# Moving the side work of a hybrid attention block: conditioning items, attention links, row sums and the last tiles of a projection

## The chip, the cores and the metric

The kernel runs on one core of a Trainium2 chip. The metric is the device time of one execution in microseconds (us), smaller is better; the time of a kernel is the median of its runs. A change of 0.3% (6.9 us here) is about what a measurement of this kernel can tell from no change.

## The reference

One layer of a streaming encoder on 512 tokens of width 2048, all in float32:

```python
c_act = silu(c)
shift_m, scale_m, gate_m, shift_f, scale_f, gate_f = split(c_act @ w_ada + b_ada, 6)
h = rmsnorm(x, g_pre_mix) * (1.0 + scale_m) + shift_m
proj = h @ w_in                 # columns: 8 attention heads, 4 gated linear heads, small ones
fox = forgetting attention of 8 heads x 128: causal softmax(q k / sqrt(128) + cum[q] - cum[k]) v
gla = gated linear attention of 4 heads (keys 128, values 256), state read at chunk ends of 64
y = concat(head_rmsnorm(fox), head_rmsnorm(gla) * silu(r)) @ w_out
x = x + gate_m * rmsnorm(y, g_post_mix)
h = rmsnorm(x, g_pre_mlp) * (1.0 + scale_f) + shift_f
x = x + gate_f * rmsnorm(square(relu(h @ w_mlp_in)) @ w_mlp_out, g_post_mlp)
```

`w_ada` is 2048 x 12288, so the conditioning vectors alone read 100 MB.

## The kernel before

It is written engine by engine in program order: every engine (SP issues the DMAs, PE multiplies, ACT is the scalar engine, DVE the vector engine, POOL the GpSimd engine) has its own list of instructions and waits on counting semaphores (`wait_ge(name, value)`). Nothing is scheduled by a planner. The order in each list is fixed by hand through tables of slots.

**Products.** Each float32 operand is split into a high part (ACT copies it to a rounded format, `split_hi`, L1101) and a low part (DVE subtracts, `split_lo`, L1485). A product is three matmuls (L737 to L739): high by high, high by low, low by high. Weights come in tiles `w_raw`, two buffers, so SP may issue tile m only once tile m-2 is split (`slot_free`).

**Groups.** The input projection is eight groups. A group has 16 steps k (eight weight tiles of two k), and a step has six column tiles b, so 288 matmuls. Groups 0 to 3 project two attention heads each, groups 4 to 7 one gated linear head each. While PE works at group r it also does the mixer of group r-1 (so attention runs in groups 1 to 4), in 32 half steps called slots: slot 2k after b=2 and slot 2k+1 after b=5 of step k (`group_steps`). ACT and DVE run the same 32 slots in `group(r, work)`; after every fourth slot they split one weight tile. The mixer of the last gated linear head has no group left: it runs in the first quarter of the output projection (`out_steps(0)`), 32 slots of two (k, t) pairs each.

**Attention (`fox_slot`).** For block j of 8 (two heads, four query blocks): PE makes logits in slot 3j (L811), DVE adds the bias and takes the row maximum (L1590 to L1595), ACT takes the exponential in slot 3j+1 (L1153), PE transposes it in 3j+2 (L821), ACT copies it in 3j+3 (L1163), PE multiplies by the values in 3j+4 (L832), DVE divides and sums squares (`f_o`, L1606, L1608), POOL takes the root (L2116), DVE normalises in 3j+6 (L1613) behind the row maximum of the next block but one, and PE transposes the result in 3j+7 (L841), ahead of the product of the next block. DVE stores it to `cat` (L1625).

**Conditioning items.** The vectors of `w_ada` that the later parts need are summed on DVE from items of 1 MB (two DMAs of 512 KB each, two buffers): eight items in each of groups 1 to 4 (`load_f` L538, `f_item` L1535), four per gated linear head (`load_g` L545, `g_item` L1552). SP's table `F_AT` says after which weight tile of a group an item is issued; DVE's table of the same name says in which slots it is added, two halves per item. SP waits for the addition of item i-2 (`am_used`) before it issues item i. At the end the partial sums are added over partitions by PE: `f_columns` (L774, 16 narrow matmuls) or `g_rows` (L780), and DVE makes the vectors of them (L1523, L1562).

**Seams.** After slot 31 DVE and ACT copy the six finished banks out (`evict_group`, L1496, L1499, L1112). PE's next group needs these copies, bank by bank. In the output projection `out_steps(cg)` takes 16 k by four token tiles t, into banks 0 to 3 and 4 to 7 in turn; in the last quarter (cg = 3) its second half goes tile by tile, so that the normalisation of tile 0 can begin early. It ends in a chain over four token tiles (L1313, L1858, L2078, L1884, L1324, L1342, L1862), before which the MLP cannot start (L1008).

## Time and profile before

| | |
|---|---|
| median of 3 runs | 2312.89 us (2312.43 to 2318.76) |
| the profiled execution: its own time | 2309.94 us |
| the profiled execution: span from first to last instruction | 2307.9 us |
| PE busy | 2173.3 us, 94% of the span |
| DVE busy | 1520.3 us, 66% |
| ACT busy | 850.8 us, 37% |
| start and group 0 | 0 to 177.8 us |
| groups 1 to 4 (with the eight attention heads) | 182.9 to 526.7 us |
| groups 5 to 7 (with three gated linear heads) | 526.7 to 753 us |
| output projection and its normalisation | 754.7 to 961.3 us |
| MLP | 961.3 us to the end |

Busy time counts computing instructions only. The idle time in front of an instruction is put down to what ended it. "PEclk" in a table of windows is the granted clock of PE: 1.00 is 2.4 GHz and 0.50 is 1.2 GHz.

### The profile page before, as it was taken

What the parts mean: (1) busy time and instruction counts of PE and PEld (TensorE: products, weight loads), DVE (VectorE), ACT (ScalarE), POOL (GpSimd) and SP (SyncE); (2) the same over time, 40 slices, a digit from 0 to 9 for tenths busy, and PEclk for the clock granted to TensorE, in tenths of its full rate; (3) what the DMA queues carried; (4) which work ended last, traced back from release to release, by engine and by line L of the source; (5) the groups of instructions that cost most, each with busy time, mean ns of one, the idle gap of its engine ahead of it and who ended that gap; (6) DMA issues with size and microseconds to landing.
All of it is one profiled execution on the core that took longest, in us unless ns stands there. A gap on an engine that the chain in (4) does not pass through costs nothing.

```text
span 2307.9 us, 26312 instructions
## 1 busy us (share of the span) xinstructions
PE 2173.3 (94%) x9751; PEld 1769.3 (77%) x9751; DVE 1520.3 (66%) x1470; ACT 850.8 (37%) x1063; POOL 385.1 (17%) x217
## 2 busy tenths in 40 slices
PE   2778999999999999799999999999999999999996
PEld 2556877777777678688888888888878888888875
DVE  5855665666667732564454454454498989898998
ACT  2223323333333322443444343343344444444443
POOL 0000000000000000100000000000034545454664
PEclk9889999999999999899999999999999999999998
DMA  9855565555545342556666566566247664666763
GB/s 314 296 186 168 170 191 178 162 175 178 164 128 173 110 164 95 165 173 196 199 223 207 193 222 215 183 220 226 92 152 247 216 208 161 239 219 218 256 221 144
DMA packets 261821, 441.09 MB, mean 191 GB/s; under 512 B 17676, under 2 KB 110032, under 8 KB 255704
## 3 DMA queue, kind: packets, MB, share of 16 engines
q1 hardware_dynamic: 261128, 435.51, 56.6%
q10 hardware_dynamic: 592, 4.21, 0.5%
q8 instruction: 66, 1.08, 0.2%
q14 instruction: 35, 0.29, 0.0%
HBM read 379.88 MB, written 59.79 MB: 191 GB/s over the span
## 4 chain that ended last, share of the span: by engine, by line
PE 78%; issue 8%; DVE 7%; DVEq 2%; DMA 1%; SPq 1%; POOL 1%; ACT 1%; POOLq 0%; ACTq 0%
PE pair L737 25%; PE pair L739 24%; PE pair L738 24%; DVE am_acc L1721 3%; DVE v_op L1940 1%; DMA af_item<-in_w_ada 1%; PE pair L832 1%; DVEq L1720 1%; PE pair L811 1%; DVE w_lo L1485 0%; DVEq L1591 0%; PE pair L926 0%; POOL v_raw L2162 0%; PE pair L1008 0%; PE pair L872 0%
## 5 line engine op out<-in xcount | busy, mean ns | idle before, releaser
L737 PE MATMUL pair<-in_hi,w_hi 128*128 128x512 f32 x1792 | 725.3, 405 | 4.5 <-DVE grp L1496 2.5
L739 PE MATMUL pair<-in_hi,w_lo 128*128 128x512 f32 x1792 | 702.8, 392 | 0.0
L738 PE MATMUL pair<-in_lo,w_hi 128*128 128x512 f32 x1792 | 702.4, 392 | 0.0
L1485 DVE TENSOR_TENSOR w_lo<-w_raw,w_hi 128x2048 fp32r<-128x2048 f32 (+1 forms) x142 | 292.1, 2057 | 397.4 <-ACT w_hi L1101 396.8
L1101 ACT ACTIVATE w_hi<-w_raw 128x2048 fp32r<-128x2048 f32 (+1 forms) x142 | 244.7, 1723 | 461.6 <-PE pair L739 424.8
L737 PEld LDWEIGHTS pair<-in_hi,w_hi 128*128 128x128 f32 x1792 | 339.6, 190 | 86.3 <-issue 12.0
L739 PEld LDWEIGHTS pair<-in_hi,w_lo 128*128 128x128 f32 x1792 | 338.6, 189 | 73.3
L738 PEld LDWEIGHTS pair<-in_lo,w_hi 128*128 128x128 f32 x1792 | 339.6, 190 | 70.2 <-issue 2.6
L737 PE MATMUL pair<-v_op,hid_r 128*128 128x512 f32 x896 | 349.8, 390 | 5.8 <-DVE hid_r L1916 4.5
L738 PE MATMUL pair<-v_op,hid_r 128*128 128x512 f32 x896 | 349.2, 390 | 0.0
L739 PE MATMUL pair<-v_op,hid_r 128*128 128x512 f32 x896 | 349.1, 390 | 0.0
L1940 DVE TENSOR_TENSOR v_op<-v_raw,v_op 128x1024 fp32r<-128x1024 f32 x192 | 302.4, 1594 | 66.4 <-ACT v_op L1464 65.2
L1464 ACT ACTIVATE v_op<-v_raw 128x1024 fp32r<-128x1024 f32 x192 | 203.6, 1061 | 295.3 <-PE pair L739 280.7
L737 PEld LDWEIGHTS pair<-v_op,hid_r 128*128 128x128 f32 x896 | 168.6, 188 | 42.5 <-issue 7.7
L739 PEld LDWEIGHTS pair<-v_op,hid_r 128*128 128x128 f32 x896 | 168.6, 188 | 35.3
L738 PEld LDWEIGHTS pair<-v_op,hid_r 128*128 128x128 f32 x896 | 168.7, 188 | 34.8
L2153 POOL TENSOR_TENSOR v_sum<-v_raw,v_raw 128x512 f32<-128x512 f32 x60 | 150.1, 2528 | 256.9 <-DVE v_raw L1955 256.9
L2162 POOL TENSOR_TENSOR v_raw<-v_raw,v_sum 128x512 f32<-128x512 f32 x64 | 145.3, 2302 | 113.4 <-POOLq L2144 95.0
L2084 POOL TENSOR_TENSOR ada<-ada,c_act 128x2048 f32<-128x2048 f32 x8 | 30.6, 3824 | 604.4 <-DMA ada<-in_w_ada 604.4
L1979 DVE TENSOR_TENSOR y_t<-pair,y_t 128x1024 f32<-128x1024 f32 x104 | 125.0, 1215 | 0.9 <-PE pair L739 0.8
L737 PE MATMUL pair<-w_hi,in_hi 128*128 128x512 f32 x256 | 102.3, 400 | 7.2 <-DVE w_lo L1485 4.2
L739 PE MATMUL pair<-w_hi,in_lo 128*128 128x512 f32 x256 | 100.4, 392 | 0.0
(205 smaller groups left out, 1880.3 us busy)
## 6 DMA issues: line engine op xcount, KB each, us to landing
w_raw<-in_w_mlp_in SPq DMA_DIRECT2D x64, 1024.0 KB, 5.3
v_raw<-in_w_mlp_out SPq DMA_DIRECT2D x128, 512.0 KB, 5.1
hid_r<-hid_scratch SPq DMA_DIRECT2D x112, 512.0 KB, 6.3
hid_scratch<-hid_r SPq DMA_DIRECT2D x28, 1792.0 KB, 7.2
am_item<-in_w_ada SPq DMA_DIRECT2D x64, 512.0 KB, 5.1
w_raw<-in_w_in SPq DMA_DIRECT2D x128, 256.0 KB, 3.4
af_item<-in_w_ada SPq DMA_DIRECT2D x64, 512.0 KB, 5.8
w_raw<-in_w_in SPq DMA_DIRECT2D x128, 128.0 KB, 3.2
```

Source lines behind the costliest of these rows:

```text
L737: pe.matmul(dst, a[0], b[0], start=start, stop=False, skip_group_check=onto)
L738: pe.matmul(dst, a[0], b[1], start=False, stop=False, skip_group_check=onto)
L739: return pe.matmul(dst, a[1], b[0], start=False, stop=stop, skip_group_check=onto)
L1101: act.activation(w_hi[n][:, view], w_raw[n][:, view], ACT.Copy).then_inc(hi_done, 1)
L1464: act.activation(v_op[i % 4][:, 0, :], raw_of(u, p)[:, h, :], ACT.Copy).then_inc(v_hi, 1)
L1485: dve.tensor_tensor(w_lo[n][:, view], w_raw[n][:, view], w_hi[n][:, view].bitcast(F32), ALU.subtract)\
L1721: last = dve.scalar_tensor_tensor(total, item, c_k, total, ALU.mult, ALU.add)
L1940: dve.tensor_tensor(v_op[i % 4][:, 1, :], raw_of(u, p)[:, h, :], v_op[i % 4][:, 0, :].bitcast(F32), ALU.subtract).then_inc(v_lo, 1)
L1979: return dve.tensor_tensor(dst, src[:, :, :], dst, ALU.add)
L2084: pool.tensor_tensor(unit[:, :, :], unit[:, :, :], c_act[:, :].rearrange("p (k o) -> p k o", o=1).to_broadcast([P, KT, P]), ALU.mult)\
L2153: last = pool.tensor_tensor(v_sum[:, h, cols], v_raw[q[B22]][:, h, cols], v_raw[q[B11]][:, h, cols], ALU.add)
L2162: last = pool.tensor_tensor(b21, b21, v_sum[:, h, cols], ALU.subtract)
```

## The change

1. SP issues the items of an attention group (1 to 4) after tiles 0, 1, 3, 3, 4, 5, 6, 7 instead of 1, 2, 4, 4, 5, 6, 7, 7, and the first two of a gated linear head after tiles 0 and 1 instead of 1 and 2. For the last head items 2 and 3 go behind tile 3 of the output projection.
2. DVE adds items in other slots (fox: 0, 1, 2, 4, 5, 8 and so on instead of 1, 2, 4, 5, 8, 10; gated linear: 2, 5, 9, 11, 15, 17, 19, 23 instead of 4, 5, 8, 9, 15, 16, 26, 28).
3. All links of the attention chain move by three slots; slots 0 and 1 hold the two transposes of the values alone, and the first bias waits in ACT's slot 2 instead of 0. The last transposed output moves from slot 28 to 31.
4. The normalisation (L1613) moves from slot 3j+6, behind a row maximum, to slot 3j+8, a slot without one.
5. The sums over partitions move: `f_columns` from slot 31 to 30, `g_rows` from 30 to 28 on PE and from 31 to 29 on DVE.
6. In the last quarter of the output projection tiles t=0 and 1 take k = 8 to 11 together, then 12 to 15; then t=2 and 3 as before. In the second quarter the banks of t=0 and 1 no longer wait for the last head.

```diff
 # SP
-            F_AT = {1: (0,), 2: (1,), 4: (2, 3), 5: (4,), 6: (5,), 7: (6, 7)}
+            F_AT = {0: (0,), 1: (1,), 3: (2, 3), 4: (4,), 5: (5,), 6: (6,), 7: (7,)}
-            G_AT = {1: 0, 2: 1, 4: 2, 5: 3}
+            G_AT = {0: 0, 1: 1, 4: 2, 5: 3}
+            G_AT_LAST = {0: (0,), 1: (1,), 3: (2, 3)}
 ...
                     if cg == 0:
-                        load_g(GLA_HEADS - 1, mm)
+                        for i in G_AT_LAST.get(mm, ()):
+                            load_g(GLA_HEADS - 1, i)
 # PE
+            def fox_value(f, half):
+                if half == 0:
                     pe.wait_ge(ev_act, 3 * f + 3)
                     pe.wait_ge(ev_dve, 3 * f + 3)
+                else:
+                    pe.wait_ge(am_col, f + F_COL)
 ...
             def fox_slot(s, f):
+                if s < 2:
+                    fox_value(f, s)
+                if s % 3 == 0 and 3 <= s <= 24:
+                    fox_logit(f, s // 3 - 1)
+                if s % 3 == 2 and 5 <= s <= 26:
+                    j = (s - 5) // 3
 ...
-                if s % 3 == 1 and 4 <= s <= 25:
-                    j = (s - 4) // 3
+                if s % 3 == 1 and 7 <= s <= 28:
+                    j = (s - 7) // 3
 ...
-                if s == 28:
+                if s == 31:
                     pe.wait_ge(fox_out, 9 * f + 8)
                     fox_out_transpose(f, 7).then_inc(fox_pv, 1)
 ...
-                if s == 30:
+                if s == 28:
                     pe.wait_ge(gla_cat, 2 * h + 1)
                     g_rows(h)
 ...
-                    if s == 31:
+                    if s == 30:
                         pe.wait_ge(fox_max, 8 * f + 8)
                         f_columns(f)
 ...
-                    steps = steps[:KT * TB // 2] + [(k, t) for t in range(TB) for k in range(KT // 2, KT)]
+                    steps = steps[:KT * TB // 2]
+                    steps += [(k, t) for k0 in (KT // 2, 3 * KT // 4) for t in range(2) for k in range(k0, k0 + KT // 4)]
+                    steps += [(k, t) for t in range(2, TB) for k in range(KT // 2, KT)]
 # ACT
-                if s == 0:
+                if s == 2:
                     act.wait_ge(cumb_in, 32 * (f + 1))
                     fox_bias(f, 0)
 # DVE
-                if s % 3 == 0 and 6 <= s <= 27:
-                    j = s // 3 - 2
+                if s in F_AT:
+                    f_item(f, *F_AT[s])
+                if s % 3 == 2 and 8 <= s <= 29:
+                    j = (s - 8) // 3
                     dve.wait_ge(fox_rstd, 8 * f + j + 1)
                     dve.tensor_scalar(f_o[:, :], f_o[:, :], f_r[:, j:j + 1], None, ALU.mult).then_inc(fox_norm, 1)
 ...
-                if s == 31:
+                if s == 29:
                     g_rows(h, rows)
```

**Place 1: SP's queue, the weight tiles of group 4 with the items of the last two attention heads** (`w_raw` is a weight tile, `cumb` the rows of the attention bias, `af_item` an item). Before:

```order
L490 DMA w_raw_74<-in_w_in 128x2x256 x2
L613 DMA cumb_96<-cum_scratch 128x512
L613 DMA cumb_97<-cum_scratch 128x512
L490 DMA w_raw_75<-in_w_in 128x2x128 x2
L490 DMA w_raw_75<-in_w_in 128x2x256 x2
L538 DMA af_item_122<-in_w_ada 128x2x512 x2
L490 DMA w_raw_74<-in_w_in 128x2x128 x2
L490 DMA w_raw_74<-in_w_in 128x2x256 x2
L538 DMA af_item_123<-in_w_ada 128x2x512 x2
```

After:

```order
L490 DMA w_raw_74<-in_w_in 128x2x256 x2
L613 DMA cumb_96<-cum_scratch 128x512
L613 DMA cumb_97<-cum_scratch 128x512
L538 DMA af_item_122<-in_w_ada 128x2x512 x2
L490 DMA w_raw_75<-in_w_in 128x2x128 x2
L490 DMA w_raw_75<-in_w_in 128x2x256 x2
L538 DMA af_item_123<-in_w_ada 128x2x512 x2
L490 DMA w_raw_74<-in_w_in 128x2x128 x2
L490 DMA w_raw_74<-in_w_in 128x2x256 x2
```

The first item stands ahead of weight tile 1 instead of behind it, the second ahead of tile 2.

**Place 2: DVE, the last gated linear head in the output projection** (`gg` is the sum of the items, `g_e` in the last but one row what PE waits for in slot 7). Before:

```order
L1637 SCALAR_TENSOR_TENSOR g_e<-g_z 128x512
L1485 TENSOR_TENSOR w_lo_79<-w_raw_75,w_hi_77 128x2048
L1641 SCALAR_TENSOR_TENSOR g_z<-g_z,g_e 128x512
L1643 SCALAR_TENSOR_TENSOR g_cum<-chunk_on,g_z 128x512
L1646 TENSOR_TENSOR g_dif<-g_cum 128x512
L1554 TENSOR_SCALAR gg<-ag_item_124,c_act 128x512
L1552 SCALAR_TENSOR_TENSOR gg<-ag_item_124,c_act,gg 128x512 x3
L1650 TENSOR_TENSOR g_e<-grp,g_dif 128x512
```

After:

```order
L1641 SCALAR_TENSOR_TENSOR g_e<-g_z 128x512
L1558 TENSOR_SCALAR gg<-ag_item_124,c_act 128x512
L1556 SCALAR_TENSOR_TENSOR gg<-ag_item_124,c_act,gg 128x512
L1489 TENSOR_TENSOR w_lo_79<-w_raw_75,w_hi_77 128x2048
L1645 SCALAR_TENSOR_TENSOR g_z<-g_z,g_e 128x512
L1647 SCALAR_TENSOR_TENSOR g_cum<-chunk_on,g_z 128x512
L1650 TENSOR_TENSOR g_dif<-g_cum 128x512
L1556 SCALAR_TENSOR_TENSOR gg<-ag_item_124,c_act,gg 128x512 x2
L1654 TENSOR_TENSOR g_e<-grp,g_dif 128x512
```

Half of the first item has moved from between `g_dif` and `g_e` to ahead of the split of the weight tile.

## Rows read from the trace of the kernel before

**Rows 1.** The page: busy time, share of the span, instructions.
```profile
PE 2173.3 (94%) x9751; PEld 1769.3 (77%) x9751; DVE 1520.3 (66%) x1470; ACT 850.8 (37%) x1063; POOL 385.1 (17%) x217
```

**Rows 2.** Waits of PE: line, releaser, us in total, times, longest us.
```profile
PE pair L841 <- DVE f_o L1613: 11.7, 4, 3.4
PE pair L1008 <- DVE y L1862: 9.9, 1, 9.9
PE pair L862 <- DVE g_e L1650: 2.9, 1, 2.9
PE pair L799 <- DVE neg_max L1595: 1.2, 1, 1.2
```

**Rows 3.** Timeline, DVE, group 3: start, us, instruction [idle before <-releaser].
```profile
384.11 1.29 DVE L1535 SCALAR_TENSOR_TENSOR af_acc<-af_item,c_act,af_acc 128x1024 f32<-128x1024 f32 x1 [4.94 <-DMA af_item<-in_w_ada]
...
387.38 0.69 DVE L1592 CUSTOM_DVE_ANT_0 logit<-pair,bias 128x512 f32<-128x512 f32 x1
...
388.23 0.28 DVE L1613 TENSOR_SCALAR f_o<-f_o,f_r 128x128 f32<-128x128 f32 x1
```

**Rows 4.** Timeline, SP's queue, same group: tiles 3 and 4, then items 2 and 3.
```profile
363.74 12.69 SPq L481 DMA_DIRECT2D w_raw<-in_w_in  x8
376.68 2.10 SPq L538 DMA_DIRECT2D af_item<-in_w_ada  x4
```

**Rows 5.** Timeline, PE, seam of groups 3 and 4: the sums, and the second tile of group 4.
```profile
440.52 1.84 PE L774 MATMUL pair<-ones,af_acc 128*128 128x1 f32 x16
...
444.02 0.50 PE L737 MATMUL pair<-in_hi,w_hi 128*128 128x512 f32 x1 [0.83 <-DVE grp L1496]
```

**Rows 6.** Windows: length, busy us (instructions) of PE, PEld, DVE, ACT, POOL, PEclk, DMA, GB/s.
```profile
216.00:218.00 2.00, 1.77 (x9) 1.70 (x10) 0.23 (x3) 1.03 (x3) 0.00 (x0) 0.62 0.91 209
218.00:220.00 2.00, 2.00 (x6) 1.59 (x5) 1.77 (x5) 0.00 (x0) 0.55 (x1) 0.53 0.54 180
...
356.40:443.30 86.90, 82.57 (x402) 66.57 (x402) 53.24 (x114) 28.16 (x47) 4.41 (x8) 1.00 0.55 170
...
755.00:760.00 5.00, 5.00 (x11) 2.15 (x9) 3.73 (x7) 0.00 (x0) 0.00 (x0) 0.58 0.63 210
760.00:765.00 5.00, 5.00 (x20) 4.08 (x19) 0.61 (x1) 4.29 (x5) 0.00 (x0) 0.74 0.00 0
```

**Rows 7.** Timeline, DVE, seam to the output projection and its slots 0 to 5.
```profile
752.27 2.29 DVE L1485 TENSOR_TENSOR w_lo<-w_raw,w_hi 128x2048 fp32r<-128x2048 f32 x1
...
759.09 0.75 DVE L1635 TENSOR_SCALAR g_z<-pair,cols_b 128x512 f32<-128x512 f32 x1 [1.19 <-PE pair L852]
...
765.57 2.29 DVE L1485 TENSOR_TENSOR w_lo<-w_raw,w_hi 128x2048 fp32r<-128x2048 f32 x1 [4.96 <-ACT w_hi L1101]
...
771.20 2.41 DVE L1552 SCALAR_TENSOR_TENSOR gg<-ag_item,c_act,gg 128x512 f32<-128x512 f32 x3
```

**Rows 8.** Timeline, PE: first matmul of the output projection, and its slot 7.
```profile
754.66 0.47 PE L737 MATMUL pair<-w_hi,in_hi 128*128 128x512 f32 x1 [1.71 <-issue]
...
774.27 0.66 PE L862 MATMUL pair<-ident,g_e 128*128 128x128 f32 x4 [2.87 <-DVE g_e L1650]
```

**Rows 9.** Timeline, PE, last k steps of cg = 0 and start of cg = 1.
```profile
809.45 0.50 PE L737 MATMUL pair<-w_hi,in_hi 128*128 128x512 f32 x1 [1.28 <-DVE in_lo L1807]
...
818.50 0.47 PE L737 MATMUL pair<-w_hi,in_hi 128*128 128x512 f32 x1 [2.40 <-DVE w_lo L1485]
```

**Rows 10.** Timeline, PE, last quarter of the output projection.
```profile
932.05 0.47 PE L737 MATMUL pair<-w_hi,in_hi 128*128 128x512 f32 x1 [1.76 <-DVE w_lo L1485]
```

**Rows 11.** Timeline, ACT, the normalisation chain of that quarter.
```profile
941.12 1.91 ACT L1324 ACTIVATE y<-x_res 128x2048 f32<-128x2048 f32 x1
```

**Rows 12.** Timeline, DVE, the same chain: the residual of token tile 0.
```profile
937.05 2.35 DVE L1884 SCALAR_TENSOR_TENSOR x_res<-y,rstd,x_res 128x2048 f32<-128x2048 f32 x1 [0.49 <-POOL rstd L2078]
```

**Rows 13.** Timeline, ACT, group 5: weight tile 1 has landed.
```profile
528.15 1.49 ACT L1101 ACTIVATE w_hi<-w_raw 128x1536 fp32r<-128x1536 f32 x1 [3.04 <-DMA w_raw<-in_w_in]
```

**Rows 14.** Timeline, PE, group 5: first matmul of weight tile 1.
```profile
537.83 0.47 PE L737 MATMUL pair<-in_hi,w_hi 128*128 128x512 f32 x1
```

More of the change, by code:

```diff
@@ L786, in ada_rows @@
                 pe.matmul(dst[:, 0:2 * P], ones[:, :], acc[:, :], start=True, stop=True).then_inc(ada_sum, 1)
-            def fox_slot(s, f):
-                if s == 0:
+            def fox_value(f, half):
+                if half == 0:
                     pe.wait_ge(ev_act, 3 * f + 3)
                     pe.wait_ge(ev_dve, 3 * f + 3)
-                    for t in range(TB):
-                        last = pe.transpose(BB[:, t * P:t * P + P], grp[:, VA, t * P:t * P + P], ident[:, :])
-                    last.then_inc(fox_v_tr, 1)
-                if s == 1:
-                    pe.wait_ge(fox_max, 8 * f + 1)
-                    for t in range(TB):
-                        last = pe.transpose(BA[:, t * P:t * P + P], grp[:, VB, t * P:t * P + P], ident[:, :])
-                    last.then_inc(fox_v_tr, 1)
-                if s % 3 == 0 and s // 3 < 8:
-                    j = s // 3
-                    i = j % TB
-                    if j:
-                        pe.wait_ge(fox_max, 8 * f + j)
-                    if j == 1:
-                        pe.wait_ge(fox_v_tok, 2 * f + 2)
-                    if j == 0:
-                        pe.wait_ge(am_col, f + F_COL)
-                    q_tile, k_tile = (QA, KA) if j < TB else (QB, KB)
-                    pe.matmul(BA[:, 0:(i + 1) * P], grp[:, q_tile, i * P:i * P + P], grp[:, k_tile, 0:(i + 1) * P],
-                              start=True, stop=True).then_inc(fox_qk, 1)
-                if s % 3 == 2 and s // 3 < 8:
-                    j = s // 3
@@ new lines, in fox_value, with fox_logit @@
+                else:
+                    pe.wait_ge(am_col, f + F_COL)
+                for t in range(TB):
+                    last = pe.transpose((BB, BA)[half][:, t * P:t * P + P], grp[:, VA + half, t * P:t * P + P], ident[:, :])
+                last.then_inc(fox_v_tr, 1)
+            def fox_logit(f, j):
+                i = j % TB
+                if j:
+                    pe.wait_ge(fox_max, 8 * f + j)
+                else:
+                    pe.wait_ge(fox_v_tok, 2 * f + 2)
+                q_tile, k_tile = (QA, KA) if j < TB else (QB, KB)
+                pe.matmul(BA[:, 0:(i + 1) * P], grp[:, q_tile, i * P:i * P + P], grp[:, k_tile, 0:(i + 1) * P],
+                          start=True, stop=True).then_inc(fox_qk, 1)
@@ L984, in out_steps @@
                             pe.wait_ge(ev_dve, GROUPS * 3)
[L985 to L986 removed]
+                            if t >= 2:
+                                pe.wait_ge(gla_cat, 2 * GLA_HEADS)
+                                pe.wait_ge(am_col, G_COL + GLA_HEADS)
                         else:
@@ L1146, in fox_slot @@
                         .then_inc(fox_v_tok, 1)
-                if s % 3 == 1 and s // 3 < 8:
-                    j = s // 3
+                if s == 2:
+                    act.wait_ge(cumb_in, 32 * (f + 1))
+                    fox_bias(f, 0)
+                if s % 3 == 1 and 4 <= s <= 25:
+                    j = (s - 4) // 3
                     n = (j % TB + 1) * P
@@ L1154, in fox_slot @@
                                    accum_out=row_sum[:, j:j + 1]).then_inc(fox_exp, 1)
-                if s % 3 == 2 and s // 3 < 7:
-                    fox_bias(f, s // 3 + 1)
-                if s % 3 == 0 and 3 <= s <= 24:
-                    j = s // 3 - 1
+                if s % 3 == 2 and 5 <= s <= 23:
+                    fox_bias(f, (s - 2) // 3)
+                if s % 3 == 0 and 6 <= s <= 27:
+                    j = s // 3 - 2
                     n = (j % TB + 1) * P
@@ L1573, in gate_row @@
                 dve.tensor_tensor(part, part, bg_bc[:, 1, :], ALU.mult).then_inc(ada_col, 1)
-            F_AT = {s: divmod(n, 2) for n, s in enumerate((1, 2, 4, 5, 8, 10, 11, 13, 14, 16, 17, 19, 22, 23, 26, 28))}
-            G_AT = {s: divmod(n, 2) for n, s in enumerate((4, 5, 8, 9, 15, 16, 26, 28))}
+            F_AT = {s: divmod(n, 2) for n, s in enumerate((0, 1, 2, 4, 5, 8, 10, 11, 13, 14, 16, 17, 20, 22, 23, 26))}
+            G_AT = {s: divmod(n, 2) for n, s in enumerate((2, 5, 9, 11, 15, 17, 19, 23))}
             def fox_slot(s, f):
-                if s % 3 == 0 and s // 3 < 8:
-                    j = s // 3
+                if s % 3 == 0 and 3 <= s <= 24:
+                    j = s // 3 - 1
                     n = (j % TB + 1) * P
@@ L1596, in fox_slot @@
                         .then_inc(fox_max, 1)
-                if s % 3 == 1 and 4 <= s <= 25:
-                    j = (s - 4) // 3
+                if s % 3 == 1 and 7 <= s <= 28:
+                    j = (s - 7) // 3
                     dve.wait_ge(fox_exp, 8 * f + j + 1)
```

16 lines of the change are left out of this document (4 added, 12 removed).

## The prediction

> **What bounds the kernel now.** The page comes first: PE is busy for 94% of the span and DVE for 66% [rows 1], so time can only be won where PE stands idle or runs at the lower clock, or by taking PE work away. The change takes none away: PE has the same matmuls before and after. The second view is the list of PE's waits [rows 2]. The first row is the pattern that the change goes for: L841, the transpose of an attention output, waits for its normalisation once in each of the four attention groups, 11.7 us in total. The other rows are single waits in the stretch that the change touches; more of them stand in the timelines [rows 8, 9, 10]. The longest, 9.9 us at L1008, is the normalisation chain in front of the MLP. The third view, the timeline of DVE, tells why L841 waits: DVE sits 4.94 us for an item to land, and only then does it split a weight tile, take a row maximum (387.38) and normalise (388.23) [rows 3]. SP's queue shows the cause of that: items 2 and 3 go out at 376.68, behind tiles 3 and 4, and item 2 lands at 384.1, 7.4 us later [rows 4]. The clock rows are read last, since a stall can cost more than its own length [rows 6].
>
> **The change part by part.** The sum is made against the profiled execution, 2309.9 us, of which 2307.9 are span. It ran 3.0 us (0.13%) below the median of the runs shown, 2312.9; I carry the saving over to that median.
>
> *Item 2 goes out earlier, and the norm leaves the slot behind the row maximum.* Item 2 now stands behind tile 3 and must wait for the addition of item 0. Counted from the end of a group's last step, T: DVE copies three banks out, adds the first half of item 0 (0.75) and splits tile 1 by about T+5.8; tile 3 takes SP until T+7.9; with the 7.4 us of [rows 4] item 2 is there at T+15.3. DVE wants it in slot 5, at about T+15 (a slot is 86.9 / 32 = 2.7 us [rows 6], and the split of tile 2 stands ahead). That is a near tie, but if the item were 2.5 us late, PE would still not notice, since the next row maximum is wanted only two slots after its logits. The transposes of outputs moreover have nearly two slots more between norm and use. So the four waits go: **-11.7 us** [rows 2]. Bounds: 0 if the late item merely stops another link, -11.7 if it goes.
>
> *Group 1.* The transposes of the second value tile no longer wait for a row maximum: -1.2 [rows 2]. After the stall in this group the granted clock fell to 0.62 and 0.53 for two windows of 2 us, in which PE was nearly always busy [rows 6]: 0.38 x 1.77 + 0.47 x 2.00 = 1.6 us. If that dip came from the stall it goes with it: **-2.8** together, between -1.2 and -2.8. By the Trainium skill (TensorE: Matmul & The Clock Gate, Part 1) idle time brings the half-rate state back, but at instants that do not follow the kernel, so one stall may be hit and the next not; the trace agrees, as group 3 with the stall of 3.4 us kept a clock of 1.00 throughout [rows 2, 6]. I count a dip only where the rows show one.
>
> *Seams of the attention groups.* The 16 narrow matmuls of the sums (1.84 us from 440.52) leave the place between the last step and the next group. PE stalls 0.83 before the second tile of that group, because DVE first makes the vectors of the sums [rows 5]. Now a single transpose stands there and DVE stores its result before it copies banks. The matmuls are not saved, only moved into slot 30; the stall should be some 0.65 instead of 0.83, as a transpose and a small store are little shorter than what they replace. Four seams: **-0.7**, between +1 and -2.5 (the whole stall gone three times).
>
> *Gated linear groups 5 to 7.* PE waits nowhere in them, so moving additions and sums earns nothing. What could be lost: item 0 now stands ahead of tile 1. Tile 1 landed at 528.15 [rows 13] and PE takes it up at 537.83 [rows 14]. The high part takes 1.5 us, the low part at most 2.3 [rows 13, 7], and DVE is busy for some 2 us between, so about 4 us of cover are left for 1 us of issue and the 1 MB of the item, 3.1 us at the rate of a full window (210 GB/s at a DMA share of 0.63 [rows 6]). I count **0**, and take the loss as a rival.
>
> *Seam to the output projection and its slots 0 to 7.* PE starts at 754.66 after 1.71 us that the profile calls issue [rows 8]; but it is the instant at which DVE's split of the first output tile ends, which started at 752.27 behind the row sums of slot 31 [rows 7]. With the sums in slot 29 that split is done before PE needs it. PE starts at 754.66 - 1.71 = 752.95. The chain of the last head then runs: PE's first product ended at 759.0 in slow clock (0.58 and 0.74 over ten microseconds [rows 6]) and would end near 755.7 without the wait of 1.7 and the 1.6 that the dip has cost by then: 3.3 us earlier. Behind it the chain (absolute value, exponential, logarithm, scan) is the same, until the four additions between scan and `g_e`, of which 771.20 shows three (2.41 us) [rows 7]: two of them move into the wait for the logarithm, 1.3 us less. So slot 7 is released about 4.6 us earlier than at 774.27, at 769.7: **-4.6**. But PE, no longer slowed, reaches slot 7 at 771.4 - 1.7 - 3.4 = 766.3 (the dip of [rows 6] costs 0.42 x 5 + 0.26 x 5 = 3.4) and stands idle for 3.4 us there, instead of 2.87 [rows 8]. Bounds: -1.3 if the dip stays, -5.9 if the chain's start hides better.
>
> *Rest of the last head.* Items 1 and 3 now stand between links that are wanted: item 3 (half) ahead of the norm of slot 20 and ahead of the stores of slots 24 and 25. I reckon 0.6 us of new stall in slot 23 and 0.8 more before k = 14 than the 1.28 of now [rows 9]. Against that the sums of slot 31 no longer hold the split for cg = 1: the 2.40 go [rows 9]. Net **-1.0**, between +1.5 and -2.4.
>
> *Last quarter.* Tile 3 of the weights is wanted after eight steps instead of four, and 1.76 us of waiting go [rows 10]. But tile t=0 ends four steps (2.8 us) later. The square of token tile 0 starts at 941.12 [rows 11], once PE has tile 1 done and ACT has squared it; its residual was there at 937.05 + 2.35 = 939.4 [rows 12]. Now tile 1 comes earlier and the residual 2.8 - 1.76 = 1.0 us later, so that it is the last, at 940.4. So the chain in front of L1008 starts only 0.7 us earlier, and the rest of the 1.8 is added to the wait of 9.9 [rows 2]: **-0.6**, between +1 and -1.8.
>
> Sum: 11.7 + 2.8 + 0.7 + 4.6 + 1.0 + 0.6 = 21.4 us. From 2309.9 that is 2288.5 for a profiled execution, from the median 2312.9 it is **2291.5 us**, 0.93% faster.
>
> **The rivals.**
> *A, the waits come back in part.* Item 2 or an item behind it is late again, or the late additions of the last head stall PE more than reckoned. For it: DVE has two halves of items and a split in some slots (16 and 17: two halves at 1.29 [rows 3] and a split, about 4.5 us with the links, against two slots of 5.4). Against: in no other slot did DVE wait for an item. Priced at half of the fox term (5.9), the output terms at 1.3 + 0, the rest as above: 5.9 + 1.2 + 0.7 + 1.3 + 0.6 = 9.7 saved, 2303 us.
> *B, more than the waits is won.* Further dips go, and the chain of the last head hides better: the outer bounds of the terms, 11.7 + 2.8 + 2.5 + 5.9 + 2.4 + 1.8 = 27.1, 2286 us.
> *C, nothing measurable.* The 11.7 us turn into the same waits elsewhere (the attention chain is only shifted, not shortened) and only the output terms remain: 5 us, 2308 us. Against: there is a named cause, the landing of one item, and it is removed.
> *D, slower.* The item ahead of tile 1 delays the tile past its cover. The Trainium skill (DMA: Bandwidth & Descriptors, Queues, rings and completion order) says that each DMA engine consumes its descriptors in ring order, so that a tile issued behind an item has to wait for it; no run here shows the tile behind the item. The place is the start of groups 4 to 7, where SP's queue is held until the first bank is copied. It decides from a delay of 4 us on (landing 528.15 against use 537.83, less two conversions [rows 13, 14]). Should tile 1 land 10 us later and the clock dip after each such stall by the 3.4 us of the dip at 755, that is 4 x (6 + 3.4) = 37.6 us lost against 21.4 won: 2329 us. Against: 1 MB needs a third of that.
>
> **How the numbers follow.** Forecast 0.60, A 0.19, B 0.10, C 0.07, D 0.04. Within 0.3% (6.9 us, about what a measurement of this kernel can tell from no change) lie C and an edge of A; faster 0.89, same 0.08, slower 0.03, as part of D would end within 0.3% too. The range goes from B's side to A's: 2284 to 2304 us.
>
> **What would show it.** Right: no wait of L841 and none of DVE for an item above 1 us in groups 1 to 4; groups 1 to 4 each some 3 us shorter than 86.9; the output projection starts directly behind group 7; a wait of 3 to 4 us at L862 in it; no wait for the split at cg = 1 and in the last quarter, but over 10 us at L1008. Wrong: waits of PE for a low part in step 2 of groups 4 to 7, waits of L821 or L811 in the attention groups, or clock below 1.00 in more places than before. That the seams still cost 0.8 each would change little.

## Result and profile after

The changed kernel takes 2289.19 us (median of 4 runs, 2288.40 to 2291.14), the kernel before beside it 2314.65 us (4 runs, 2312.43 to 2318.76). The ratio is 0.9889, 95% interval 0.9872 to 0.9906: 1.1% faster, and within the range that was forecast. The profiled executions were 2309.94 us before and 2288.4 us after, with spans of 2307.9 and 2286.3 us, so the profiles show 21.6 us of saving, against a sum of 21.4. The medians show 25.5 (2314.65 less 2289.19): the profiled execution before was 4.7 us below its median, the one after 0.8 below. Only mean clocks are on record for the runs without a profile, so where the other 4 us lie isn't shown. The parts below are those of the two profiles.

The page of the changed kernel, its header and the busy times, to hold against [rows 1]:

```profile
span 2286.3 us, 26308 instructions
PE 2166.9 (95%) x9751; PEld 1766.9 (77%) x9751; DVE 1521.4 (67%) x1470; ACT 850.9 (37%) x1063; POOL 389.4 (17%) x217
```

PE's busy time fell by 6.4 us although it runs the same matmuls. Over the whole execution 4.1 us of that are less time at 1.2 GHz (windows of 2 us, busy time multiplied by one minus the clock): the stretches at 216 us (1.6) and from 754 to 764 us (3.4) are gone, but the one behind the first waits of group 1, from 181 us on, costs 2.8 us in this profile and cost 1.4 in the one before. The waits say where the rest went. PE's waits in the changed kernel, the main ones from ahead of group 1 to the MLP (us in total, times, longest):

```profile
PE pair L1012 <- DVE y L1866: 10.7, 1, 10.7
...
PE pair L863 <- DVE g_e L1654: 2.9, 1, 2.9
PE pair L955 <- DVE f_z L1804: 2.9, 1, 2.9
PE pair L739 <- DVE grp L1500: 2.5, 3, 0.8
...
PE pair L739 <- DVE in_lo L1811: 2.1, 1, 2.1
PE pair L739 <- DVE w_lo L1489: 1.6, 1, 1.6
PE pair L858 <- ACT gv_tok L1186: 1.5, 2, 0.8
...
PE pair L891 <- DVE g_o L1691: 0.4, 1, 0.4
```

The four waits of the output transpose (L841 before, L842 now) and the L799 wait of [rows 2] have no row any more. The row of 9.9 us is now 10.7 (L1012). L858 is new: the transposes of the gated values wait for ACT in groups 6 and 7.

DVE in group 3 of the changed kernel; the second row is item 2, the third a block's norm in a slot of its own:

```profile
361.42 1.76 DVE L1489 TENSOR_TENSOR w_lo<-w_raw,w_hi 128x1536 fp32r<-128x1536 f32 x1 [0.65 <-ACT w_hi L1105]
363.34 1.28 DVE L1539 SCALAR_TENSOR_TENSOR af_acc<-af_item,c_act,af_acc 128x1024 f32<-128x1024 f32 x1 [0.17 <-issue]
...
369.51 0.28 DVE L1619 TENSOR_SCALAR f_o<-f_o,f_r 128x128 f32<-128x128 f32 x1
```

The wait of 4.94 us for the item in [rows 3] is gone. DVE still waits for items in two other groups, 3.13 us for item 1 in group 1 (190.84) and this for item 2 in group 4:

```profile
448.07 1.28 DVE L1539 SCALAR_TENSOR_TENSOR af_acc<-af_item,c_act,af_acc 128x1024 f32<-128x1024 f32 x1 [1.72 <-DMA af_item<-in_w_ada]
```

PE waits for nothing behind either. To see how much each stretch gave, I take four landmarks on PE, first in the kernel before, then in the changed one: the transposes ahead of group 1, the first matmul of the gated chain in group 5 and in the output projection, and the transposes ahead of the MLP.

```profile
180.91 0.41 PE L954 MATMUL pair<-ident,f_z 8*128 8x8 f32 x4 [2.89 <-DVE f_z L1800]
529.67 1.12 PE L852 MATMUL pair<-ga_t,a2h 16*128 16x512 f32 x2
756.98 2.07 PE L852 MATMUL pair<-ga_t,a2h 16*128 16x512 f32 x2
961.30 1.94 PE L1008 MATMUL pair<-ident,y 128*128 128x128 f32 x8 [9.94 <-DVE y L1862]
```

```profile
180.17 0.41 PE L955 MATMUL pair<-ident,f_z 8*128 8x8 f32 x4 [2.89 <-DVE f_z L1804]
514.82 1.12 PE L853 MATMUL pair<-ga_t,a2h 16*128 16x512 f32 x2
740.82 1.12 PE L853 MATMUL pair<-ga_t,a2h 16*128 16x512 f32 x2
940.25 2.15 PE L1012 MATMUL pair<-ident,y 128*128 128x128 f32 x9 [10.70 <-DVE y L1866]
```

The differences between neighbouring rows are the columns of this table; the last column is the same for all and is left out of the argument. The other kernels' landmarks were read in the same way.

| kernel | groups 1 to 4 | groups 5 to 7 and the seam | output projection | from the MLP on |
|---|---|---|---|---|
| before | 348.8 | 227.3 | 204.3 | 1346.6 |
| after | 334.7 | 226.0 | 199.4 | 1346.1 |
| after, second profile | 334.6 | 226.0 | 199.4 | 1345.9 |
| item order alone | 337.8 | 227.5 | 204.3 | 1346.4 |
| norm's slot alone | 340.6 | 227.1 | 204.3 | 1346.0 |
| gated tables back | 335.3 | 227.1 | 206.3 | 1346.1 |
| two items ahead of tile 1 | 334.4 | 235.6 | 199.4 | 1346.1 |
| seam and quarter back | 334.1 | 225.9 | 200.7 | 1346.5 |
| five edits more | 326.7 | 224.2 | 194.1 | 1345.8 |

In the last row the first landmark stands 3 us inside group 1, as that version makes these transposes there. The first column holds the low clock at the start of group 1 too: 1.4 us before, 2.5 to 2.9 in every other kernel but the last (none). So it tells 1.2 to 1.5 us too little for each edit of the kernel before.

Before against after: 14.1 us in the attention groups, 1.3 in groups 5 to 7, 4.9 in the output projection, together 20.3. The rest (0.7 ahead of group 1, 0.6 in the MLP) the change doesn't touch; the part ahead of group 1 ended anywhere between 179.0 and 183.0 us in these profiles.

### The profile page after: what moved, and what is told of

It is laid out like the page before. It is cut to its first block, busy times and chain, and to the rows that moved or that the text cites. A ratio compares the mean times of both kernels' runs of the same rounds, so it can differ in the third digit from the quotient of the medians.

```text
span 2286.3 us, 26308 instructions
## 1 busy us (share of the span) xinstructions
PE 2166.9 (95%) x9751; PEld 1766.9 (77%) x9751; DVE 1521.4 (67%) x1470; ACT 850.9 (37%) x1063; POOL 389.4 (17%) x217
## 4 chain that ended last, share of the span: by engine, by line
PE 80%; issue 8%; DVE 7%; DVEq 1%; SPq 1%; POOL 1%; ACT 1%; DMA 1%; POOLq 0%; ACTq 0%
PE pair L739 25%; PE pair L741 25%; PE pair L740 25%; DVE am_acc L1725 3%; DVE v_op L1944 1%; PE pair L833 1%; PE pair L807 1%; DVEq L1724 1%; DVE w_lo L1489 1%; DMA w_raw<-in_w_in 0%; PE pair L927 0%; POOL v_raw L2166 0%; PE pair L1012 0%; PE pair L824 0%; SPq L563 0%
## 5 line engine op out<-in xcount | busy, mean ns | idle before, releaser
L739 PEld LDWEIGHTS pair<-in_hi,w_hi 128*128 128x128 f32 x1792 | 339.2, 189 | 85.7 <-issue 12.0
L2120 POOL TENSOR_TENSOR f_r<-f_ms,neg_half 128x1 f32<-128x1 f32 x32 | 23.4, 732 | 461.4 <-DVE f_ms L1612 461.4
```

Of the source, the lines that this page charges most:

```text
L739: pe.matmul(dst, a[0], b[0], start=start, stop=False, skip_group_check=onto)
```

## Experiments

**The item's place alone** (on the kernel before):

```diff
-            F_AT = {1: (0,), 2: (1,), 4: (2, 3), 5: (4,), 6: (5,), 7: (6, 7)}
+            F_AT = {1: (0,), 2: (1,), 3: (2,), 4: (3,), 5: (4,), 6: (5,), 7: (6, 7)}
```

> The kernel before; the only edit is on SP's queue in the attention groups: item 2 is issued behind tile 3 and item 3 behind tile 4, where both stood behind tile 4. No slot of any engine is moved. Theory (the late landing of item 2 is the cause of the four L841 waits): DVE no longer waits 4.9 us for the item, the four L841 waits (11.7 us) go, and with them the L799 wait or the low clock at 216 us at most in part; time 2311 - 11.7 = about 2300 us, between 2298 and 2302, and no L841 row above 1 us in the list of PE's waits. Rival (the order of work in DVE's slots is the cause, a row maximum ahead of a normalisation that PE wants one slot later): the waits shrink to 1 to 2 us each, time 2304 to 2308 us. Rival (nothing): 2311 us.

Measured: 2296.11 us against 2313.35 for the kernel before, ratio 0.993 (0.9911 to 0.995). That is 17.2 us less, below the 2298 to 2302 that was expected; the two profiled executions (2309.94 and 2298.29) are 11.7 apart, and what the other runs gained on top isn't shown. No L841 row is left. PE's waits of this kernel, two of the rows that stayed:

```profile
PE pair L737 <- DVE grp L1496: 2.5, 3, 0.8
...
PE pair L799 <- DVE neg_max L1595: 1.4, 1, 1.4
```

By the table the move of one DMA issue is worth 11.0 of the 14.1 us of the attention part. The late landing is the cause, and the four waits were priced rightly. The other 3.1 us are the L799 wait (1.4) and a dip of the clock (1.6). The dip, though, is not where it was. In the kernel before it began at 216.4 us, directly behind the L841 wait of group 1; the L799 wait had ended 26 us earlier, and the clock stayed at 1.00 behind it:

```profile
190.40 0.66 PE L799 MATMUL pair<-ident,grp 128*128 128x128 f32 x4 [1.15 <-DVE neg_max L1595]
...
216.23 0.30 PE L841 MATMUL pair<-ident,f_o 128*128 128x128 f32 x1 [3.09 <-DVE f_o L1613]
```

Windows of this kernel, columns: window, length, busy time of each engine, granted clock, DMA share, GB/s:

```profile
216.00:218.00 2.00, 2.00 (x12) 1.66 (x11) 1.88 (x2) 0.64 (x2) 0.55 (x1) 1.00 0.00 2
...
268.00:270.00 2.00, 1.16 (x5) 0.74 (x4) 1.78 (x4) 1.35 (x2) 0.00 (x0) 0.88 0.93 324
270.00:272.00 2.00, 2.00 (x8) 1.50 (x7) 0.26 (x1) 1.71 (x2) 0.00 (x0) 0.50 1.08 384
272.00:274.00 2.00, 2.00 (x10) 1.81 (x9) 0.70 (x4) 0.60 (x1) 0.00 (x0) 0.76 1.06 381
```

With the L841 wait gone the clock stays at 2.4 GHz there. Now the first seam's stall of 0.84 us (PE, 269.12) is followed by 1.2 GHz, and that costs the same 1.6 us.

**The norm's slot alone** (on the kernel before, DVE):

```diff
-                if s % 3 == 0 and 6 <= s <= 27:
-                    j = s // 3 - 2
+                if s % 3 == 2 and 5 <= s <= 26:
+                    j = (s - 5) // 3
                     dve.wait_ge(fox_rstd, 8 * f + j + 1)
```

> The kernel before; the only edit is on DVE: the normalisation of an attention output moves from slot 3j+6, behind the row maximum, to slot 3j+5, ahead of that slot's item addition. SP's order stays, so DVE still waits some 4.9 us for item 2 in each attention group. Theory (cause is the landing; the norm's own slot only takes PE's output transpose out of its way): no L841 wait, but DVE is still late with the split of tile 2 and the row maximum behind the item, and PE waits for these instead (L821, the transposes of probabilities, or L739 for a low part), 0.5 to 2.5 us in each of four groups; time 2301 to 2309 us. Rival (the norm's place alone was the cause): all 11.7 us go, 2299 us, and no new wait takes their place.

Measured: 2303.74 us (8 runs, 2298.72 to 2305.99), ratio 0.9958 (0.9944 to 0.9971). The profiled execution is the fastest of the eight, 5 us below their median. PE's waits show what took the place, and DVE and PE in group 3 show how:

```profile
PE pair L821 <- DVE f_o L1606: 2.5, 3, 1.0
```

```profile
373.05 0.28 DVE L1613 TENSOR_SCALAR f_o<-f_o,f_r 128x128 f32<-128x128 f32 x1 [0.67 <-POOL f_r L2116]
377.10 1.28 DVE L1535 SCALAR_TENSOR_TENSOR af_acc<-af_item,c_act,af_acc 128x1024 f32<-128x1024 f32 x1 [3.77 <-DMA af_item<-in_w_ada]
...
381.92 0.34 DVE L1606 TENSOR_SCALAR f_o<-pair,row_inv 128x128 f32<-128x128 f32 x1
```

DVE still waits for item 2 (3.77 us), but the norm is done before it, so PE's transpose of outputs runs. What is late next is the division (381.92), and PE's transposes of probabilities wait for it, 0.8 us on average in three groups. So the two causes are in series: the norm's slot only takes the victim out of the way. It gives 8.2 us by the table (two seams met the low clock in this profile, 1.6 us each), and the item order gives 11.0; the change makes both, and on these waits the second adds nothing to the first.

**The gated tables undone** (on the changed kernel; SP's tables, DVE's slots 4, 5, 8, 9, 15, 16, 26, 28, and the row sums in slots 30 and 31 as before):

```diff
-            G_AT = {0: 0, 1: 1, 4: 2, 5: 3}
-            G_AT_LAST = {0: (0,), 1: (1,), 3: (2, 3)}
+            G_AT = {1: 0, 2: 1, 4: 2, 5: 3}
+            G_AT_LAST = {0: (0,), 1: (1,), 2: (2,), 3: (3,)}
```

> The changed kernel with its gated linear part undone: items of these groups behind tiles 1, 2, 4, 5 as before, their additions in the old slots, the sums of the rows on PE in slot 30 and on DVE in slot 31 again. The attention part and the last quarter stay changed. Theory (5.6 us of the saving stand at the seam to the output projection and in the last head, less 1.5 us that item 0 ahead of tile 1 costs in groups 6 and 7): the stall of 1.7 us at the start of the output projection, that of 2.4 us at cg = 1 and a slower last head come back, the two waits at L858 go; time 2289.2 + 4.1 = about 2293 us, between 2291 and 2298 (the latter if the low clock at 755 us comes back too). Rival (that part brought nothing of its own, the attention groups all): 2289 us.

Measured: 2296.57 us, ratio 0.9932 (0.9913 to 0.9952), so 7.4 us more than the changed kernel (9.9 by the two ratios, 11.0 by the profiles, whose execution was the slowest of the four), at the upper end of what was expected. PE in the output projection of this kernel, and two windows behind the second row:

```profile
742.75 0.47 PE L739 MATMUL pair<-w_hi,in_hi 128*128 128x512 f32 x1 [1.71 <-issue]
...
761.27 1.11 PE L863 MATMUL pair<-ident,g_e 128*128 128x128 f32 x4 [4.34 <-DVE g_e L1654]
...
808.15 0.76 PE L739 MATMUL pair<-w_hi,in_hi 128*128 128x512 f32 x1 [2.40 <-issue]
```

```profile
762.00:764.00 2.00, 2.00 (x7) 1.61 (x6) 1.85 (x3) 1.57 (x2) 0.00 (x0) 0.50 0.85 294
...
808.00:810.00 2.00, 1.85 (x5) 1.49 (x6) 2.00 (x5) 0.27 (x1) 0.00 (x0) 0.50 0.35 44
```

The waits of 1.71 and 2.40 us are back to the hundredth, and the one at slot 7 is 1.4 longer than in either kernel, as this time PE was not slowed on its way there. Summed over the rows of the list these waits are 3.1 us more than in the changed kernel (10.0 against 6.9, the L858 wait of 1.5 being gone). Another 4.4 us are low clock that followed the waits of 4.34 and 2.40 us (2.8 at 760 to 768 us and 1.6 at 808 to 812, each window's busy time multiplied by one minus its clock). Together that is 7.5 of the 8.0 us by which the second and third columns of the table differ.

**Two items ahead of tile 1** (on the changed kernel, to size rival D):

```diff
-            G_AT = {0: 0, 1: 1, 4: 2, 5: 3}
+            G_AT = {0: (0, 1), 4: (2,), 5: (3,)}
...
-                    if mm in G_AT:
-                        load_g(h, G_AT[mm])
+                    for i in G_AT.get(mm, ()):
+                        load_g(h, i)
```

> The changed kernel; the only edit is on SP's queue in the gated linear groups: item 1 is issued with item 0 ahead of tile 1, where it stood behind tile 1. Theory (a tile behind an item on the same queue lands later by the item's issue and transfer; the first item already used up the cover): tile 1 lands 3 to 5 us later again in each of three groups, and PE waits 3 to 5 us more at L858 (its copy stands behind the tile's split on ACT) or for the low part at L739 in groups 5 to 7: 9 to 15 us, time 2298 to 2304 us, more if the clock dips after these stalls. Rival (the item shares the queues and does not delay the tile; the new waits at L858 have another cause): 2289 to 2290 us.

Measured: 2301.07 us, ratio 0.9953 (0.9937 to 0.9968), 11.9 us more than the changed kernel (14.8 by the two ratios, 10.7 by the profiles). The L858 row grows to this:

```profile
PE pair L858 <- ACT gv_tok L1186: 6.9, 3, 3.7
```

The same wait in three kernels, group 6: ACT takes up tile 1 and PE the values' transposes, first in the changed kernel, then here. In the kernel before, ACT started on that tile at 604.82, the instant of PE's first gated matmul (604.80); in the changed kernel it is 4.0 us behind it (589.76), here 7.1 behind (591.24).

```profile
593.78 1.49 ACT L1105 ACTIVATE w_hi<-w_raw 128x1536 fp32r<-128x1536 f32 x1 [6.04 <-DMA w_raw<-in_w_in]
...
598.31 0.66 PE L858 MATMUL pair<-ident,grp 128*128 128x128 f32 x4 [0.61 <-ACT gv_tok L1186]
```

```profile
598.36 1.48 ACT L1105 ACTIVATE w_hi<-w_raw 128x1536 fp32r<-128x1536 f32 x1 [9.13 <-DMA w_raw<-in_w_in]
...
602.88 1.12 PE L858 MATMUL pair<-ident,grp 128*128 128x128 f32 x4 [3.70 <-ACT gv_tok L1186]
```

Each megabyte ahead of the tile delays it: the first by 3.1, 4.0 and 4.7 us in groups 5, 6 and 7, the second by 2.1, 3.1 and 2.1. The Trainium skill (DMA: Bandwidth & Descriptors, Queues, rings and completion order) has descriptors of one ring consumed in order, and this agrees. The second item costs 5.4 us in waits and 4.0 in low clock behind them (600 and 682 us).

**The seam and the last quarter undone** (on the changed kernel; PE's side is shown, DVE's `f_columns` moves back from slot 30 to 31 likewise):

```diff
-                    if s == 30:
+                    if s == 31:
                         pe.wait_ge(fox_max, 8 * f + 8)
                         f_columns(f)
...
-                    steps = steps[:KT * TB // 2]
-                    steps += [(k, t) for k0 in (KT // 2, 3 * KT // 4) for t in range(2) for k in range(k0, k0 + KT // 4)]
-                    steps += [(k, t) for t in range(2, TB) for k in range(KT // 2, KT)]
+                    steps = steps[:KT * TB // 2] + [(k, t) for t in range(TB) for k in range(KT // 2, KT)]
```

> The changed kernel with two small parts undone, far from each other, so that one profile shows both: the sums of the columns stand in slot 31 of the attention groups again, on PE and DVE, and the last quarter of the output projection takes the token tiles in the order of before. Theory: at the seams the stall of 0.83 us before the second tile stays what it is (it is DVE's first copy behind another small operation, whichever that is), so groups of 82.0 us, plus or minus 0.2; in the last quarter 1.8 us of waiting for the low part of tile 3 come back and the wait ahead of the MLP falls from 10.7 to 9.9, so 0.5 to 1.0 us more; time 2289 to 2291 us. Rival (the sums in slot 30 shortened the seams): 0.5 to 1.8 us more per attention group, 2292 us or more. Rival for the quarter (the chain in front of the MLP is bound by PE's last tile alone): 1.8 us more, and the wait ahead of the MLP stays at 10.7.

Measured: 2288.62 us, ratio 0.9899 (0.9879 to 0.9919); the changed kernel on the same chip 2287.78. PE's waits:

```profile
PE pair L1010 <- DVE y L1864: 9.9, 1, 9.9
...
PE pair L739 <- DVE w_lo L1487: 3.3, 2, 1.8
...
PE pair L739 <- DVE grp L1498: 2.5, 3, 0.8
```

The seams cost 2.5 us in three groups with either order, the one behind group 4 costs 0.4 us instead of 0.6, and the attention groups take 334.1 us instead of 334.6. Moving these sums brought nothing. The quarter is as expected: 1.8 us of waiting for the low part are back and the last wait is 0.8 shorter, so the new order is worth 1.0 us (1.3 by the table).

**The changed kernel again:**

> The changed kernel as it is, on the same chip as the others of this call, for a direct comparison: 2289 us, 2287 to 2293. All theories expect the same; what it tells is how far one kernel's profile moves from run to run, the places of low clock above all: the theory that a low clock hangs on idle stretches expects them at the same places as in the first profile (152, 180, 930, 1664 us), and at some of the 0.8 us stalls of the seams in one run and not in the next.

Measured: 2287.78 us (2287.29 to 2289.96), with the same waits to within 0.1 us between group 1 and the MLP, and the same dips (near 152, 180, 930 and 1664 us). At the seams neither of the two profiles has one, where the expectation had them in one run and not in the next.

**A version with five edits more** (a part of it is shown; left out are PE's transposes ahead of group 1, which go into its slot 0, ACT's side of (2) and (5), and DVE's slots for the items of (3) and for items and reciprocals of (4)):

```diff
 # DVE: (1) first bank ahead of slot 31's store; (2) group 0's banks inside the forget-gate chain
+                    if s == 4 * MM_G - 1 and first_evict:
+                        first_evict()
                     work(s)
...
+            split_lo(MM_G, 0, NARROW)
...
+            evict_group(0, True)
             dve.wait_ge(fz_ln, 1)
# SP, (3)
-            G_AT = {0: 0, 1: 1, 4: 2, 5: 3}
+            G_AT = {1: 0, 2: 1, 4: 2, 5: 3}
# DVE, last head, (4)
-                if s % 8 == 2 and s // 8 + 1 < MM_O:
+                if s in (3, 10, 18):
# DVE, (5)
-                if t >= 2:
-                    scale_x1(t - 1)
+            scale_x1(1)
             dve.wait_ge(x1_ss, TB + 1)
...
+            scale_x1(2)
             scale_x1(TB - 1)
```

> An attempt to beat the changed kernel, five edits to it. (1) Attention seams: DVE copies its first bank before the store of slot 31; the three stalls of 0.83 us should go (2.5 us, and the low clock that a run may show behind one). (2) Start of group 1: the first weight tile is split and the banks of group 0 are copied around the forget-gate chain, not behind it, and PE's transposes of its result move from ahead of group 1 into its slot 0; of 2.9 + 1.6 us of waiting 0.3 to 0.6 us are left, and the low clock at 180 us (2.8 us) may go. (3) Gated groups: item 0 behind tile 1 again, its additions in slots 4 and 6; the two waits at L858 (1.5 us) go. (4) Last head: DVE splits the weight tile behind the scan chain, the reciprocals go into its idle stretch (slots 8 and 14) and one addition behind the sums of squares; 2.9 us at slot 7, 0.4 at slot 23 and 2.1 ahead of k = 14 go. (5) Chain in front of the MLP: two scalings on DVE and a weight split on ACT stand behind the last token tile's residual and squares; the wait of 10.7 us shrinks to about 9.0. Theory (each of these waits is the last thing late at its place): 2.5 + 4.0 + 1.5 + 5.4 + 1.7 = 15.1 us less than the changed kernel, about 2274 us, 2270 to 2277 with the clock. Rival (the next link is close behind: copies, the landing of the broadcast rows, another low part): half of it, 2281 us. Rival (something in the reordered start is held longer): no gain, 2287 us or more.

Measured: 2274.24 us, ratio 0.983 (0.9814 to 0.9846), 13.5 us less than the changed kernel on the same chip, where the theory had 15.1: inside its range. Up to the second landmark the profile gains 7.9 us (506.90 against 514.82), then 1.8 in groups 5 to 7 and 5.3 in the output projection. Between group 1 and the MLP these are all of PE's waits:

```profile
PE pair L1018 <- DVE y L1884: 10.3, 1, 10.3
...
PE pair L824 <- ACT prob L1163: 1.4, 2, 1.0
...
PE pair L891 <- DVE g_o L1704: 1.0, 1, 1.0
```

Two places fell short. L891 still waits 1.0 us for a norm that stands behind an addition. And the wait ahead of the MLP shrank by 0.4 instead of 1.7. POOL and DVE there:

```profile
921.90 1.15 POOL L2098 TENSOR_SCALAR ms<-ss_x 128x1 f32<-128x1 f32 x1 [0.23 <-DVE ss_x L1910]
```

```profile
921.73 1.28 DVE L1884 TENSOR_SCALAR y<-x_res,rstd 128x2048 f32<-128x2048 f32 x1
923.78 1.29 DVE L1884 TENSOR_SCALAR y<-x_res,rstd 128x2048 f32<-128x2048 f32 x1 [0.78 <-POOL rstd L2100]
```

The scaling that I had moved there runs from 921.73 to 923.01, and POOL's instruction, one number per partition, ends at 923.05. The last version tries that reading.

**Two of these places changed again** (PE's waits for the scaled tiles and ACT's splits of the first two MLP tiles move to suit, not shown):

```diff
 # ACT, instead of DVE's scale_x1(2)
+            act.wait_ge(x1_rstd, 3)
+            act.activation(y[:, 2, :], x_res[:, 2, :], ACT.Copy, scale=rstd[:, 6:7]).then_inc(xn2_ready, 1)
# DVE, additions of the last head
-            G_AT_LAST = {s: divmod(n, 2) for n, s in enumerate((2, 6, 9, 11, 15, 18, 19, 23))}
+            G_AT_LAST = {s: divmod(n, 2) for n, s in enumerate((2, 6, 9, 11, 15, 18, 20, 23))}
```

> The version x1_all with two places changed again, where its profile fell short. (1) In the chain in front of the MLP POOL's two small instructions for the last token tile took 1.15 and 0.55 us, the first beginning beside a scaling on DVE (921.73 to 923.01) and ending with it (923.05); alone it takes 0.19. Now ACT does the scaling of token tile 2 and DVE has nothing between the sum of squares and the last scaling; ACT splits the first MLP tile ahead of the last squares, as in the changed kernel. (2) The addition of slot 19 stands behind the norm of slot 20. Theory (a POOL instruction that starts while DVE scales is held until DVE has ended): the first POOL instruction behind the last sum takes 0.2 us, the last scaling starts 1.0 to 1.2 us behind that sum where it was 2.1, the wait ahead of the MLP goes from 10.3 to 9.8 or 10.0, the wait of 1.0 us at L891 goes: about 1.5 us less than x1_all, 2272 to 2273 us. Rival (POOL's long instructions there have another cause): the POOL instruction stays above 1 us and only the 1.0 us of L891 are won.

> The version x1_all as it is, on the same chip as x2_more, for a direct comparison: 2272 to 2276 us. If the low clock hangs on idle stretches, it shows none between 178 and 900 us again, as all stalls over 1.1 us in that stretch are gone.

Measured: 2273.51 us, ratio 0.9821 (0.9803 to 0.9838), beside 2274.86 us, 0.9824 (0.9806 to 0.9841), for the version before it. The two medians differ by less than a measurement tells, but the profile shows both edits. POOL, then PE's wait:

```profile
920.74 0.19 POOL L2100 TENSOR_SCALAR ms<-ss_x 128x1 f32<-128x1 f32 x1 [0.66 <-DVE ss_x L1913]
```

```profile
PE pair L1018 <- DVE y L1887: 9.7, 1, 9.7
```

With DVE idle POOL's instruction takes 0.19 us, the last scaling starts 1.2 us behind the sum instead of 2.1, and the L891 row is gone. This version has the lowest median: it is 1.8% faster than the kernel before and 0.7% faster than the changed one by their ratios. All three profiles of these two versions show no dip of the clock from 178 to 900 us; in that of the second run of the version before it this holds although PE waited 1.32 us at L824 in group 4 (447.92), so not all stalls over 1.1 us were gone as expected.

## Why the prediction was right, and where it wasn't

**The four waits, -11.7 us: right.** 11.7 went; the item order alone gives 11.0 in the attention part, with 1.6 of low clock at a seam standing in the old one's place. Rival C (the chain is only shifted) falls: with no slot moved the waits go. The near tie was one: in groups 2 and 3 nothing holds DVE at the addition of item 2 but 0.17 us of issue, in group 4 it waits 1.72 us for it, and PE doesn't notice, as forecast. The sign "none of DVE for an item above 1 us" did not hold, but the 3.1 us in group 1 and the 1.7 in group 4 cost PE nothing. Groups 2 and 3 now take 82.0 us from seam to seam, before 85.2 and 85.7; the 86.9 of [rows 6] is a window somewhat longer than a group.

**Group 1, -2.8: right in total, with the wrong link.** The wait of 1.2 and the dip of 1.6 are both absent, but I had tied the dip to that wait. It began 26 us later, directly behind the L841 wait of 3.09 us in the same group, so it went with the first term's wait and not with this one. With the L799 wait kept (1.4 us) the clock stayed up behind it, and it fell behind a seam's 0.84 instead. In the eight profiles that have these stalls it fell behind neither of the two L799 waits, behind one of the four L841 waits, and behind 3 of 24 seam stalls of 0.8 us (once with the item order, twice with the norm's slot). By these counts a dip behind a stall is a chance, and a forecast that books one as certain has luck in it. The attention part gained 14.1 us where these two terms say 14.5: the dip at its start cost 1.4 us more in the profile after, and 1.0 us more was won that stands in no row of the waits.

**Seams, -0.7: wrong, 0.** The stall is 0.85 instead of 0.83 at each of three seams, at the fourth it was 0.4 all along and is 0.6 now, and undoing the move changes nothing for the three. The step that failed is "the stall should be some 0.65": it subtracted the lengths of two small operations. What holds PE is that DVE's first copy stands behind any operation that waits for PE's last transpose. With the copy ahead of that operation the row is gone.

**Gated groups 5 to 7, 0: wrong, +1.5 us of waits (1.0 by the landmarks, less the 1.7 of issue and 0.6 of low clock at the seam).** The delay was sized rightly (4.1 us forecast, 3.1 to 4.7 measured). The cover was not 4 us. I counted tile 1's own path, its split and PE's use, and left out what is queued behind that split on ACT: the exponential, a table load of 1.28 us, the logarithm and the copy of the values, for which PE waits in slot 3. That is rival D's mechanism at a twenty-fifth of its price; the second item shows how quickly it grows once cover is gone (5.4 us of waits, 9.4 with the clock).

**Seam to the output projection and slots 0 to 7, -4.6: right.** Group 7 runs straight into the projection. Slot 7 is released 16.4 us behind the end of the group (739.36 to 755.74), before it was 21.3 (752.95 to 774.27), so 4.9 earlier; the wait there is 2.93, forecast 3.4.

**Rest of the last head, -1.0: right, -1.2.** The 2.40 at cg = 1 went; 0.39 at slot 23 (forecast 0.6) and 2.09 instead of 1.28 ahead of k = 14 (forecast 0.8 more) came: 2.40 - 0.39 - 0.81 = 1.2.

**Last quarter, -0.6: right in sign and mechanism, -1.0.** 1.76 of waiting went and the wait ahead of the MLP grew from 9.94 to 10.70, so it gave back 0.8 where I had 1.1.

That the sum was met to 0.2 us is in part luck. By the table the attention part gave 1.1 less than forecast (14.1 for 15.2, seams included) and the gated groups 1.0 less; the last head with its seam and the quarter gave 0.9 more (0.3 + 0.2 + 0.4), and 1.3 came outside the change, which is noise. Against the medians the saving was forecast 4 us too small. The price of the part of the change in the gated tables would have been told too low by the waits alone: undone, it costs 3.1 us of waits and 4.4 of clock.

## What to carry to other kernels

When an engine waits for a late transfer, look first at where its issue stands in the queue: one line in SP's table gave 11 of the 22 us here (by the profiles), and reordering the waiting engine around it gave less and left a new wait. When something is issued ahead of a tile, count the cover not up to the tile's use, but up to the first user of anything that is queued behind the tile's conversion. After such a step read the list of waits to the end: the small rows that were left (0.8 at each seam, 2.9 and 1.6 ahead of group 1, 1.5 in the gated groups, 2.9, 2.1 and 0.4 in the last head) were worth 13.5 us more, the clock behind them included. A dip of the clock belongs to the stall that ends right before it: look for that row before pricing it with another.

## What the chip showed that I had not expected

**The clock.** Of the stalls ahead of group 1 (2.9 and 1.6 us, one matmul group of 0.41 between them) every profile that has them (eight) shows 1.2 GHz behind them, between 178 and 192 us. The first windows of the changed kernel, and then one of the version with five more edits at the same place:

```profile
180.00:182.00 2.00, 0.41 (x4) 0.33 (x4) 1.97 (x3) 1.72 (x5) 0.00 (x0) 0.67 0.05 8
182.00:184.00 2.00, 1.86 (x4) 1.49 (x5) 1.80 (x4) 1.99 (x2) 0.00 (x0) 0.50 0.31 96
...
186.00:188.00 2.00, 2.00 (x9) 1.67 (x8) 1.60 (x2) 0.60 (x1) 0.00 (x0) 0.62 0.95 318
```

```profile
182.00:184.00 2.00, 2.00 (x12) 1.65 (x12) 0.00 (x0) 1.99 (x3) 0.00 (x0) 1.00 0.29 98
```

The dip is worth 2.8 us here (2.5 to 2.9 in seven profiles, 1.4 in that of the kernel before) on top of the 4.5 that the list of waits shows. A single stall of 2.93 us in the output projection brought none in either profile of the changed kernel, and one of 3.38 in group 3 none in the kernel before; one of 3.09 in group 1 did there, and one of 0.84 did in the item-order kernel: length alone doesn't decide. The Trainium skill (TensorE: Matmul & The Clock Gate, Part 1) has idle time bring back the half rate at instants that don't follow the kernel, and these rows agree.

**POOL beside DVE.** The same POOL instruction on one number per partition took 0.19 us with DVE idle (so it did in the kernels before and after) and 1.15 when it started during DVE's scaling of 128x2048, and it ended with that. The Trainium skill (SBUF — State Buffer, SBUF: two separate sides) has DVE and GpSimd share one pair of ports under an exclusive lock held for a whole instruction; by its page VectorE: DVE Perf Modes (Mode 2×_2P) a float32 scaling from SBUF to SBUF uses both of DVE's ports. The two runs agree with that. A small POOL link in a chain can thus cost what is left of a DVE scaling that it starts beside.

What stays open: why the clock falls behind one seam and not the next, where the 4 us lie by which the medians gained more than the profiles, and the 1.4 us at L824 in group 1 that came when the start was reordered (its bias rows and item 1 land later relative to the group; not tried).
